# High and low parts of the activations side by side in TensorE's form products, with the weight sums made by accumulating transfers

## The reference

```python
def rms_norm(x, g):
    y = x * lax.rsqrt(jnp.mean(x * x, axis=-1, keepdims=True) + EPS)
    return y * g
def swiglu(h, wg, wu, wd):              # wg, wu: 1024 x 2816, wd: 2816 x 1024
    return (jax.nn.silu(h @ wg) * (h @ wu)) @ wd
for layer in range(2):
    x = x + 0.5 * swiglu(rms_norm(x, ffn_norm[layer, 0]), ...)
    x = x + mixer(rms_norm(x, mix_norm[layer]))
    x = x + 0.5 * swiglu(rms_norm(x, ffn_norm[layer, 1]), ...)
```

## Time and profile before

| | us |
|---|---|
| median of 3 runs (lowest, highest) | 1691.17 (1691.09, 1691.37) |
| the profiled execution's own time | 1690.82 |
| its span in the trace | 1689.0 |
| PE busy | 1674.9 |
| DVE busy | 1285.5 |
| ACT busy | 753.4 |
| POOL busy | 121.2 |

### The profile page before, as it was taken

One profiled execution on the slowest core, in us unless ns is written; L12 is line 12 of the kernel. 1 busy time (PEld: TensorE's weight loads), 2 busy tenths in 40 slices (PEclk: granted clock), 3 DMA queues, 4 the chain that ended last, 5 costly groups with the idle time before them and its releaser, 6 DMA issues.

```text
span 1689.0 us, 25810 instructions
## 1 busy us (share of the span) xinstructions
PE 1674.9 (99%) x10644; PEld 1492.2 (88%) x10644; DVE 1285.5 (76%) x1466; ACT 753.4 (45%) x1008; POOL 121.2 (7%) x115
## 2 busy tenths in 40 slices
PE   8999999999999999999999999999999999999999
PEld 7899999987876688999999889999998889999997
DVE  6977877767788658887877687877876798778774
ACT  7434435443237555444434464434434644344341
POOL 0010300032014220000000200000001000000000
PEclk9999999999999999999999999999999999999999
DMA  7422422162420034332421443422411334224212
GB/s 219 141 85 76 150 76 87 63 149 71 102 66 26 14 100 138 112 113 75 131 95 38 126 125 101 138 87 76 150 38 65 106 117 147 79 76 149 75 58 68
DMA packets 180924, 165.05 MB, mean 98 GB/s; under 512 B 15396, under 2 KB 156680, under 8 KB 180808
## 3 DMA queue, kind: packets, MB, share of 16 engines
q1 hardware_dynamic: 179960, 162.79, 30.8%
q10 hardware_dynamic: 848, 0.61, 0.2%
HBM read 160.89 MB, written 2.10 MB: 96 GB/s over the span
## 4 chain that ended last, share of the span: by engine, by line
PE 92%; DVE 5%; issue 1%; ACT 1%; DMA 0%; SPq 0%; DVEq 0%; ACTq 0%
PE ps_s L747 19%; PE ps_s L749 19%; PE ps_s L748 19%; PE ps_y L747 6%; PE ps_y L748 6%; PE ps_y L749 6%; PE ps_stat L747 2%; PE ps_aux L747 2%; PE ps_aux L749 2%; PE ps_stat L749 2%; PE ps_aux L748 2%; PE ps_stat L748 2%; PE ps_s L1153 1%; PE ps_y L1182 1%; PE ps_aux L1202 1%
## 5 line engine op out<-in xcount | busy, mean ns | idle before, releaser
L747 PE MATMUL ps_s<-xg_hi,w_hi 128*128 128x256 f32 (+1 forms) x1280 | 409.7, 320 | 1.3 <-DVE w_lo L1793 1.3
L749 PE MATMUL ps_s<-xg_hi,w_lo 128*128 128x256 f32 (+1 forms) x1280 | 406.6, 318 | 0.0
L748 PE MATMUL ps_s<-xg_lo,w_hi 128*128 128x256 f32 (+1 forms) x1280 | 406.6, 318 | 0.0
L1793 DVE TENSOR_TENSOR w_lo<-raw,w_hi 128x1024 fp32r<-128x1024 f32 (+2 forms) x210 | 252.8, 1204 | 135.9 <-ACT w_hi L1333 135.7
L747 PE MATMUL ps_s<-xt_hi,w_hi 128*128 128x256 f32 x1152 | 326.2, 283 | 2.1 <-ACT pair_gu L1333 2.1
L748 PE MATMUL ps_s<-xt_lo,w_hi 128*128 128x256 f32 x1152 | 326.0, 283 | 0.0
L749 PE MATMUL ps_s<-xt_hi,w_lo 128*128 128x256 f32 x1152 | 326.0, 283 | 0.0
L1333 ACT CAST w_hi<-raw 128x1024 fp32r<-128x1024 f32 (+1 forms) x212 | 217.7, 1029 | 183.6 <-PE ps_s L749 78.3
L747 PEld LDWEIGHTS ps_s<-xg_hi,w_hi 128*128 128x128 f32 x1280 | 243.9, 191 | 21.2 <-issue 3.5
L748 PEld LDWEIGHTS ps_s<-xg_lo,w_hi 128*128 128x128 f32 x1280 | 243.9, 191 | 18.6 <-issue 1.4
L749 PEld LDWEIGHTS ps_s<-xg_hi,w_lo 128*128 128x128 f32 x1280 | 243.8, 190 | 16.5
(11 more groups left out here) (369 smaller groups left out, 2386.3 us busy)
## 6 DMA issues: line engine op xcount, KB each, us to landing
scratch<-in_ffn_w_down SPq DMA_DIRECT2D x64, 512.0 KB, 4.7
raw<-in_ffn_w_gate SPq DMA_DIRECT2D x48, 512.0 KB, 4.0
raw<-in_ffn_w_up SPq DMA_DIRECT2D x48, 512.0 KB, 6.1
raw_b<-in_ffn_w_gate SPq DMA_DIRECT2D x40, 512.0 KB, 4.9
raw_b<-in_ffn_w_up SPq DMA_DIRECT2D x40, 512.0 KB, 6.9
raw<-in_hyb_w_in SPq DMA_DIRECT2D x18, 512.0 KB, 3.8
raw<-in_ffn_w_down SPq DMA_DIRECT2D x8, 768.0 KB, 5.5
raw_b<-in_ffn_w_down SPq DMA_DIRECT2D x8, 768.0 KB, 5.3
```

The source lines that it names most:

```text
L747: mm(bank, hi, x_hi, start=first, stop=False, **kw)
L748: mm(bank, hi, x_lo, start=False, stop=False, **kw)
L749: return mm(bank, lo, x_hi, start=False, stop=last, **kw)
L1793: tt(shaped(weight(w_lo, n, 0, BLOCKS[n] * P)), source, shaped(f32(weight(w_hi, n, 0, BLOCKS[n] * P))), ALU.subtract).then_inc(lo_ready, 1)
```

## The change

1. **Products.** `xg_hi` and `xg_lo` become one tensor `xg`, likewise `xt`. A block of a form is one product of 512 columns (weight high part by [x high | x low]) and one of 256 (weight low part by x high), added into the right half. The two halves of the result have to be added later. A form fills two banks in place of one: even forms banks 0 and 1, odd forms 2 and 3, in every step.
2. **Folding.** A snapshot is 128x1024 (into unused columns of `xg`); each `add_to` becomes three DVE operations of 128x512 (two in `begin_sum`, one in `end_sum`), `scale_last` three in place of one.
3. **Weight sums.** Those of steps 3 to 10 leave DVE. ACT negates two quarters (`negate`, 2 x 128x1024) and POOL issues four accumulating transfers of 512 KB inside SBUF, one after the other (`form_sums`). Those of step 2 stay on DVE. POOL's angle passes of ffn 0 stand between these transfers. The weights of a step lie by quarters, loaded in eight transfers of 256 KB.
4. **Order.** In `first_pairs` the high part of the fourth product moves behind the first snapshot (`last_high`), up tiles 2 and 3 go to `ps_y`, form 0 of step 2 waits for the fourth gate tile (before, for the third), and ffn 0 and 3 have a new order. In `x_forms` signs change, and no operation is added.

```diff
-            xg_hi = sb("xg_hi", [P, KD * T], F32R, before_output)
+            xg = sb("xg", [P, 2 * KD * T], F32R, before_output)
         out_rows = sb("out_rows", [P, NQ, D])
-        xg_lo = sb("xg_lo", [P, KD * T], F32R)
+        behind_output = sb("behind_output", [P, KD * T])
+        out_flat = out_rows[:, :, :].rearrange("p q d -> p (q d)")
...
+        def parts_of(ap):
+            return ap[:, :].rearrange("p (l c) -> p l c", l=2)
+        def form_banks(m):
+            return ps_s[:, 2:4, :] if m in (1, 3, 5) else ps_s[:, 0:2, :]
+        def plain_bank(f, up):
+            return ps_y[:, f % 2, :] if up and f >= 2 else ps_s[:, 2 * up + f % 2, :]
+        def kept(m):
+            rows = behind_output[:, 0:4 * T] if m == 2 else out_flat[:, 0:4 * T]
+            return rows.rearrange("p (j l c) -> p j l c", j=2, l=2)[:, :, :, 0:H]
...
-                bank = ps_s[:, s % 2 + 2 * (m in (1, 3, 5)), :]
-                if m < 2 and s < FIRST + 2:
-                    pe.wait_ge(up_scaled if m else gate_scaled, 4 * ffn + s + 1)
+                if m == 0 and s == FIRST:
+                    pe.wait_ge(gate_scaled, 4 * ffn + 4)
+                elif m == 1 and s == FIRST:
+                    pe.wait_ge(up_scaled, 4 * ffn + 2)
                 elif m == 0:
-                    pe.wait_ge(last_scaled, q - 1)
+                    pe.wait_ge(last_folded, q)
                 elif m == 1:
-                    pe.wait_ge(added, 3 * q - 3)
+                    pe.wait_ge(added, 3 * q)
...
                 pe.wait_ge(lo_ready, n + 1)
                 for j in range(2):
+                    bank = form_banks(m)[:, j, :]
                     for k in range(4):
-                        if m in (0, 1, 5):
-                            at = (k + 4 * (m > 0)) * T + (0 if m == 5 else H)
-                            x_hi, x_lo = xg_hi[:, at:at + H], xg_lo[:, at:at + H]
-                        else:
-                            t = {3: 0, 2: 1, 4: 2, 6: 3}[m]
-                            x_hi, x_lo = quarters_of_x(xt_hi)[:, t, k, :], quarters_of_x(xt_lo)[:, t, k, :]
+                        x_at = (k + 4 * (m > 0)) * T + (0 if m == 5 else H)
+                        t_at = ({2: 1, 4: 2, 6: 3}.get(m, 0) * 4 + k) * H
+                        x_both = parts_of(xg)[:, :, x_at:x_at + H] if m in (0, 1, 5) else parts_of(xt)[:, :, t_at:t_at + H]
                         at = (4 * j + k) * P
-                        last_mm = three(bank[:, j * H:(j + 1) * H], weight(w_hi, n, at, at + P), weight(w_lo, n, at, at + P),
-                                        x_hi, x_lo, m in (0, 1, 3) and j == 0 and k == 0, j == 1 and k == 3,
-                                        skip_group_check=True)
+                        mm(parts_of(bank), weight(w_hi, n, at, at + P), x_both, start=m in (0, 1, 3) and k == 0, stop=False,
+                           skip_group_check=True)
+                        last_mm = mm(bank[:, H:T], weight(w_lo, n, at, at + P), x_both[:, 0, :], start=False, stop=k == 3,
+                                     skip_group_check=True)
                 last_mm.then_inc(unit_done, 1)
...
+            def negate(ffn, s):
+                act.wait_ge(step_landed[(s - FIRST) % 2], step_landed_by(ffn, s))
+                a21 = quarter_row(s, 1, 0)
+                nc.scalar.activation(a21, a21, ACT.Copy, scale=-1.0).then_inc(negated, 1)
+                act.wait_ge(lo_ready, u_form(ffn, s - 1, 3) + 1)
+                if s - 1 == FIRST:
+                    act.wait_ge(s_made, 4 * ffn + 3)
+                else:
+                    act.wait_ge(s_summed[(s - 1) % 2], summed_by(ffn, s - 1, 3))
+                nc.scalar.activation(s1, quarter_row(s, 1, 1), ACT.Copy, scale=-1.0).then_inc(negated, 1)
...
+            def last_high(ffn):
+                act.wait_ge(a_ready, 4 * ffn + 4)
+                copy(tile_of(turn_hi, 3), work[:, 1, :]).then_inc(act_hi_ready, 1)
...
-            def snapshot(ffn, s, m, dst):
+            def snapshot(ffn, s, m):
+                q = q_of(ffn, s)
                 act.wait_ge(unit_done, u_form(ffn, s, m) + 1)
-                copy(dst, ps_s[:, s % 2 + 2 * (m == 3), :].rearrange("p (m c) -> p m c", m=2)).then_inc(snapped, 1)
+                at_least(act, folded, 3 * q + (1 if m == 3 else 0))
+                copy(kept(m), form_banks(m).rearrange("p j (l c) -> p j l c", l=2)).then_inc(snapped, 1)
             def step(ffn, s):
                 q, n = q_of(ffn, s), u_form(ffn, s, 0)
                 if s > FIRST:
                     split(n + 2)
+                split(n + 3)
+                snapshot(ffn, s, 0)
                 if s == FIRST:
-                    act.wait_ge(xt_lo_ready, 2 * ffn + 2)
-                else:
-                    act.wait_ge(pair_product, q)
-                snapshot(ffn, s, 0, pair_gu[:, :, 0, H:T])
-                split(n + 3)
+                    last_high(ffn)
                 split(n + 4)
-                snapshot(ffn, s, 2, pair_gu[:, :, 0, 0:H])
+                if s < LAST:
+                    negate(ffn, s + 1)
+                snapshot(ffn, s, 2)
                 split(n + 5)
-                snapshot(ffn, s, 3, pair_gu[:, :, 1, 0:H])
                 split(n + 6)
+                snapshot(ffn, s, 3)
                 split(n + 7)
...
+                    split(n + 8)
+                    gate_of(2)
+                    sum_1(ffn)
+                    sum_3(ffn)
+                    up_of(2)
+                    split(n + 9)
+                    product_of(2)
+                    sum_2(ffn)
+                    low_of(2)
+                    split(n + 10)
+                    gate_of(3)
+                    up_of(3)
+                    sum_4(ffn)
...
-            def add_to(ffn, s, m, dst):
+            def begin_sum(ffn, s, m, dst):
+                q, of = q_of(ffn, s), {1: 0, 4: 3, 5: 2}[m]
                 dve.wait_ge(unit_done, u_form(ffn, s, m) + 1)
-                dve.wait_ge(snapped, 3 * q_of(ffn, s) + {1: 1, 4: 3, 5: 2}[m])
-                tt(dst, in_halves(ps_s[:, s % 2 + 2 * (m != 4), :]), dst, ALU.add).then_inc(added, 1)
+                dve.wait_ge(snapped, 3 * q + {0: 1, 2: 2, 3: 3}[of])
+                at_least(dve, pair_product, q)
+                tt(dst, form_banks(m)[:, :, 0:H], kept(of)[:, :, 0, :], ALU.add).then_inc(half_folded, 1)
+                dve.wait_ge(half_folded, 3 * q + {1: 1, 4: 2, 5: 3}[m])
+                tt(dst, form_banks(m)[:, :, H:T], dst, ALU.add).then_inc(added, 1)
+            def end_sum(ffn, s, m, dst):
+                count = 3 * q_of(ffn, s) + {1: 1, 4: 2, 5: 3}[m]
+                dve.wait_ge(added, count)
+                tt(dst, kept({1: 0, 4: 3, 5: 2}[m])[:, :, 1, :], dst, ALU.add).then_inc(folded, 1)
+                dve.wait_ge(folded, count)
             def scale_last(ffn, s):
+                q, dst = q_of(ffn, s), pair_gu[:, :, 1, H:T]
                 dve.wait_ge(unit_done, u_form(ffn, s, 6) + 1)
-                tt(pair_gu[:, :, 1, H:T], in_halves(ps_s[:, s % 2, :]), rstd_of(H, 2), ALU.mult).then_inc(last_scaled, 1)
+                at_least(dve, pair_product, q)
+                nc.vector.tensor_copy(dst, form_banks(6)[:, :, 0:H]).then_inc(last_begun, 1)
+                dve.wait_ge(last_begun, q + 1)
+                tt(dst, form_banks(6)[:, :, H:T], dst, ALU.add).then_inc(last_folded, 1)
+                dve.wait_ge(last_folded, q + 1)
+                tt(dst, dst, rstd_of(H, 2), ALU.mult).then_inc(last_scaled, 1)
...
+                c11, c12, c22 = pair_gu[:, :, 0, H:T], pair_gu[:, :, 0, 0:H], pair_gu[:, :, 1, 0:H]
                 if s > FIRST:
                     add_half(ffn, s - FIRST - 1, 1)
                     split(n + 2)
                 split(n + 3)
-                add_to(ffn, s, 1, pair_gu[:, :, 0, H:T])
+                begin_sum(ffn, s, 1, c11)
                 split(n + 4)
-                dve.wait_ge(added, 3 * q + 1)
-                c11 = pair_gu[:, :, 0, H:T]
+                end_sum(ffn, s, 1, c11)
                 tt(c11, c11, rstd_of(H, 2), ALU.mult).then_inc(pair_scaled, 1)
                 split(n + 5)
+                split(n + 6)
+                begin_sum(ffn, s, 4, c22)
+                split(n + 7)
+                end_sum(ffn, s, 4, c22)
+                begin_sum(ffn, s, 5, c12)
+                end_sum(ffn, s, 5, c12)
+                split(n + 8)
                 if s < LAST:
-                    sum_1(ffn, s + 1)
-                split(n + 6)
-                if s < LAST:
-                    sum_3(ffn, s + 1)
-                add_to(ffn, s, 4, pair_gu[:, :, 1, 0:H])
-                split(n + 7)
-                add_to(ffn, s, 5, pair_gu[:, :, 0, 0:H])
-                dve.wait_ge(added, 3 * q + 3)
+                    split(n + 9)
                 left = pair_gu[:, :, :, 0:H]
                 tt(left, left, rstd_of(0, 2, 2), ALU.mult).then_inc(pair_scaled, 1)
-                split(n + 8)
                 scale_last(ffn, s)
                 if s < LAST:
```

(27 more changed lines are left out.)

218 lines of the change are left out of this document (136 added, 82 removed).

## The result

The changed kernel takes 1706.97 us (median of 4 runs, 1705.62 to 1707.45); the kernel before took 1691.13 (median of 4) in the same comparison. The ratio is 1.0095, 95% interval 1.0083 to 1.0107: 0.95% slower. The forecast was 1682, the range ended at 1697. The profiled execution took 1707.05, its span is 1705.2 us against 1689.0: 16.2 us more.

What follows compares the result with a forecast made beforehand. PE's sequence was taken to bound the kernel. Products -26.9, FFN starts +6.0 and step 10 ends +11.8 gave -9.1 us, from a profiled 1690.82 to 1681.7, forecast as 1682 us; range 1672 to 1697.

Steps and rivals of the forecast that it cites:

- Sum: Whole kernel: product saving, late starts and step 10 ends add to -26.9 + 6.0 + 11.8 = -9.1 us, giving 1682 us.
- Products: PE's forms: a block falls from 0.360 to 0.2267 + 0.120 = 0.3467 us, saving 26.9 us over 2016 blocks.
- A normal step: Steps away from FFN starts and ends: no stall, ACT and DVE hidden under PE, a step 30.3 us.
- The transfers: POOL's accumulating weight sums: 6 us each assumed, bounds 4 and 14; PE waits only above 8.0, or the third above 10.8.
- The end of step 10: PE in last_round waits 3.1 us for DVE's late chain where it waited 0.18, four times: 11.8 us lost.
- The starts: FFN starts: form 0 waits for the fourth gate tile; 2.6 us lost in ffn 0 and 3, 0.4 in 1 and 2, together 6.0.
- (b): Rival: a 512-column product reading two runs costs as two, 0.240 us, so no saving: 1709 us, chance 0.04.
- (a): Rival: the accumulating transfers land late and PE waits; at 10 us each +192 us, some 1874 us; chance 0.15.

Runs made afterwards that it cites:

- e3: Changed kernel with spare products, whose results nobody reads, filling PE's waits ahead of form 0 in ffn 0 and 3 and in each last_round: 1696.04 us.
- e4: Kernel before, with four dependent 512-column copies (2.9 us) on DVE ahead of form 6's scaling in step 10 of each FFN: 1708.66 us.
- e12: Changed kernel with early gate tile, filled last round, form 1 folded earlier in ffn 0 and 3, and products grouped eight 512s then eight 256s: 1672.37 us.
- e1: Changed kernel with each block's first product reading one run of 512 neighbouring columns in place of two runs of 256: 1705.75 us.
- e8: Changed kernel with the 256-column product adding into the left half of the bank, not the right: 1703.91 us.
- e9: Changed kernel with the second product of each block also 512 columns wide, so widths no longer alternate: 1899.83 us.
- e2: Changed kernel with each bank's products reordered, four of 512 columns and then four of 256: 1698.31 us.

## Why the prediction was wrong

Its sum was -26.9 + 6.0 + 11.8 = -9.1. The span grew by 16.2, 25.3 us away. Two steps failed.

**The sum left out what follows a wait** (under "Sum"). The prediction made PE wait at six places, for lengths that came out nearly right, and took each wait at its own length. Behind or from within five of the six PE ran at 1.2 GHz for 3.4 or 6.8 us. e3 keeps the lateness and fills the waits: -10.9 us. e4 adds such waits to the old kernel: the clock falls behind all four. The runs give the price: 10.9 us for waits of 21 us. The Trainium skill, TensorE: Matmul & The Clock Gate (HAM oscillation), tells of a kernel whose TensorE waited between short bursts and came back at half clock each time; the runs here agree with it in kind. I had read that page for its issue gap only.

**The price of a block, 0.2267 + 0.120 = 0.3467** (under "Products"). Each width's distance had been read in a run of its own width. Mixed one by one a pair costs 0.353, and so the products save 36 x (20.15 - 19.77) = 13.7 us in the forms and not 26.9; about 1 us of that goes again, since the half units between them take 10.94 us in place of 10.91. The bounds were two runs free or two runs dear, and neither had anything to say on widths. The row that I used to dismiss it, a 512 ahead of a 256 in the earlier trace rows, is a single change, and in the harmless direction. What costs is the first 512s behind 256s, and the kernel before shows that too, where its half units begin:

```profile
143.02 0.40 PE L748 MATMUL ps_y<-turn_lo,w_hi 128*128 128x512 f32 x1
143.26 0.39 PE L749 MATMUL ps_y<-turn_hi,w_lo 128*128 128x512 f32 x1
```

From 142.79 on its first five products stand 234, 236, 229, 232 and 231 ns apart, then 227 (medians over its rounds), while the first 256 behind a 512 is followed after 113 and not 120. Groups of eight (e12) show the same: 233, 236, 228, 232, 231, then 227, and 113 for the first 256. One by one it is 236 for every 512 and 117 for every 256.

e1, e8 and e9 leave the alternation as the cause: not the two runs, not the place in the bank, not the product itself. e2 and e12 show it fading with fewer changes: 0.353 with 2 changes a block, 0.3504 with half a one, 0.3486 with a quarter. Over 0.3467 that is 6.3, 3.7 and 1.9 ns: 7.4 or 7.6 a change in groups of four or eight, but 3.2 one by one, where the five dear products don't fit between two changes. What in the engine does this stays open.

The rest, by its own steps:

- **A normal step.** Right: no wait of PE in steps 3 to 8 and 10; only form work of step 9 of ffn 0 is 0.4 us longer. Step 30.71 and not 30.3, by the block price.
- **The transfers.** Right in that PE never waits for them, but with little to spare. From the first issue to the third landing it takes 22.3 us (median, at most 23.6), where the prediction left 32.7 - 8.7 = 24.0, and the third lands up to 2.1 us after form 0 of the next step, where 32.7 - 30.3 = 2.4 was the limit. That the median of 6.1 meets the assumed 6 is luck: it is that of a mixture. The estimate by the Trainium skill, DMA: Bandwidth & Descriptors, had been 3.2 to 4.4; a transfer with nothing beside it takes 4.5, close to the 4.4 for two sources, one beside loads 6.1 to 10.3, which the trace shows and the estimate doesn't.
- **The end of step 10.** Right in mechanism, place and size: 3.03 us of waiting for the predicted 3.1, (3.03 - 0.18) x 4 = 11.4 for 11.8.
- **The starts.** Mechanism right, size off. Form 0 was to start 3.3 us late and came 5.1 us late in ffn 0 and 4.8 in ffn 3, since the split ahead of the gate tile hangs by ACT on DVE's third sum, a loop that the working had not followed. Some of it comes back, as form 2 waited 1.3 us in the kernel before as well. From e3, where no clock mixes in, counted from the start of the last plain product: ffn 0 loses 5.1 ahead of form 0, gets 1.3 back and loses 0.3 inside the forms (20.05 us for 19.77), 4.1 in all for the predicted 2.6; ffn 3 4.8 - 1.3 + 0.5 = 4.0; ffn 1 and 2 lose 0.2 each for the predicted 0.4. With the 0.4 us of step 9 that makes 8.9 for 6.0.
- **Left out, on the gaining side.** Before, PE waited for a split amid the plain units of ffn 0 and of ffn 3 (0.8 us at 48.20 and 0.5, by the profile). In the new order of DVE both are gone, 1.1 and 0.7 us by the starts of the products.

The account of the 16.2 us, in spans: products -13.7 + 1.0, ends 11.4, starts 8.9, waits gone -1.8, clock 10.0 (1705.2 less e3's 1695.2): 15.8. The other 0.4 us is that in e3's execution the first plain products start so much later than before; from one execution to the next they differ by that and more.

None of the rivals was the cause. (b) priced a block too high and is refuted by e1; that its 1709 lies near the measured 1707 is chance. (a), which held most of the chance for slower, never showed.
